# Two edits in the expert phase: a multiply moves from VectorE to Pool, and a reload moves from SyncE's queue to ScalarE's

## The reference, cut to what matters

```python
def block(xc):                                    # 128 tokens at a time
    q = (xc @ w_q).reshape(PEER_BLOCK, PEER_HEADS, 2, PEER_KEY_DIM // 2)
    s = jnp.einsum("chsd,hskd->chsk", q, keys)
    top_s, top_i = lax.top_k(s, PEER_TOPK)
    ...                                           # the best 16 of 16 x 16 pairs, for each of 8 heads
    e = i1 * PEER_NKEYS + i2                      # 128 of 16384 experts per token
    g = jax.nn.softmax(best_s, axis=-1)
    act = jax.nn.gelu(jnp.einsum("cd,chkd->chk", xc, u_tab[e]))
    return jnp.einsum("chk,chkd->cd", g * act, v_tab[e])

x = x + g_f * peer_ffn(modulate(rmsnorm(x, norm_ffn_w[i]), sh_f, sc_f), ...)
```

## Time and profile before

| | |
|---|---|
| time, median of 3 runs | 3000.66 us (2999.98 to 3004.64) |
| the profiled execution's own time | 2996.64 us |
| its span, first to last instruction | 2994.8 us |
| granted TensorE clock, mean | 0.946 |
| busy share: TensorE, VectorE, Pool, ScalarE | 88%, 70%, 42%, 24% |
| moved by DMA | 917.84 MB, mean 306 GB/s |
| of it by the gathers' queue / the queue of plain DMAs | 536.94 MB / 378.73 MB |

### The profile page before, as it was taken

The page is one execution under the profiler, slowest core; times in us unless marked ns, Lnnn a source line. Parts: engine busy times, 40 slices in busy tenths (PEclk is TensorE's granted clock), DMA queues, the critical chain, the costliest instruction groups (busy, mean ns, idle before and its releaser), DMA issues. The chain is left out here.

```text
span 2994.8 us, 36163 instructions
## 1 busy us (share of the span) xinstructions
PE 2631.8 (88%) x12550; PEld 2163.9 (72%) x12550; DVE 2099.4 (70%) x4541; ACT 706.4 (24%) x1947; POOL 1246.7 (42%) x1028
## 2 busy tenths in 40 slices
PE   4789869999999996999966878999999998899993
PEld 2544558888888885888854756888888886688882
DVE  2365248989979866666674346989989976666666
ACT  2345142234444300000004424213444410000000
POOL 0000000546557765555650000164656765556662
PEclk7888989999999998999987988999999999899996
DMA  7156122899999999999991213499999999999995
GB/s 297 64 216 266 56 100 65 326 349 367 360 375 409 408 409 404 409 409 409 409 365 63 77 56 121 148 385 323 369 362 409 408 407 406 408 409 409 409 409 205
DMA packets 246587, 917.84 MB, mean 306 GB/s; under 512 B 27120, under 2 KB 32272, under 8 KB 239120
## 3 DMA queue, kind: packets, MB, share of 16 engines
q0 software_dynamic: 147456, 536.94, 45.9%
q1 hardware_dynamic: 98960, 378.73, 33.0%
HBM read 909.27 MB, written 6.29 MB: 306 GB/s over the span
## 5 line engine op out<-in xcount | busy, mean ns | idle before, releaser
L1093 POOL DMA_INDIRECT all_xT<-in_u_rows,peer_eidx x296 | 375.7, 1269 | 1127.2 <-DVE peer_eidx L1436 879.0
L1164 PE MATMUL exp_down<-peer_gates,all_ring 128*128 128x256 f32 x2720 | 619.7, 385 | 72.3 <-DMA all_ring<-in_peer_v 72.1
L1164 PEld LDWEIGHTS exp_down<-peer_gates,all_ring 128*128 128x128 f32 x2720 | 512.0, 191 | 170.0 <-DMA all_ring<-in_peer_v 102.2
L1136 PE MATMUL exp_out<-peer_hd,all_ring 128*128 128x256 f32 x2752 | 616.0, 380 | 12.6 <-DMA all_ring<-in_uT 6.6
L1136 PEld LDWEIGHTS exp_out<-peer_hd,all_ring 128*128 128x128 f32 x2752 | 516.5, 190 | 89.9 <-DMA all_ring<-in_uT 14.3
L1518 DVE SCALAR_TENSOR_TENSOR peer_hs<-all_xT,peer_dots,peer_hs 128x1024 f32<-128x1024 f32 x226 | 290.5, 1285 | 144.5 <-DMA all_xT<-in_peer_v,peer_eidx 141.4
L1511 DVE CUSTOM_DVE_ANT_0 all_xT<-all_xT,peer_hs 128x1024 f32<-128x1024 f32 x296 | 359.5, 1220 | 42.7 <-DMA all_xT<-in_u_rows,peer_eidx 41.6
L1093 POOL DMA_INDIRECT all_xT<-in_peer_v,peer_eidx x228 | 261.7, 1148 | 178.4 <-DVE peer_hs L1518 154.2
L1164 PE MATMUL exp_down<-peer_gates,spare_ring 128*128 128x256 f32 x1376 | 314.4, 381 | 8.2 <-DMA spare_ring<-in_peer_v 8.2
L1136 PE MATMUL exp_out<-peer_hd,spare_ring 128*128 128x256 f32 x1344 | 305.5, 380 | 8.0 <-DMA spare_ring<-in_uT 4.4
L1164 PEld LDWEIGHTS exp_down<-peer_gates,spare_ring 128*128 128x128 f32 x1376 | 257.8, 190 | 53.8 <-DMA spare_ring<-in_peer_v 19.2
(11 more groups left out here) (293 smaller groups left out, 3700.8 us busy)
## 6 DMA issues: line engine op xcount, KB each, us to landing
all_ring<-in_uT SPq DMA_DIRECT2D x172, 512.0 KB, 6.8
all_ring<-in_peer_v SPq DMA_DIRECT2D x170, 512.0 KB, 6.8
mix_raw<-in_ada_tiles SPq DMA_DIRECT2D x48, 1024.0 KB, 9.8
spare_ring<-in_peer_v SPq DMA_DIRECT2D x86, 512.0 KB, 6.8
spare_ring<-in_uT SPq DMA_DIRECT2D x84, 512.0 KB, 6.7
all_ring<-in_w_peer_q SPq DMA_DIRECT2D x22, 512.0 KB, 3.8
all_ring<-in_w_gs_in SPq DMA_DIRECT2D x16, 512.0 KB, 3.7
all_ring<-in_w_in SPq DMA_DIRECT2D x12, 512.0 KB, 3.8
```

The source lines that it names most:

```text
L1093: nc.gpsimd.indirect_dma_start(out=rows[j], out_offset=None, in_=table, in_offset=bass.IndirectOffsetOnAxis(ap=q.eidx[:, b, k:k + 1], axis ...
L1136: mm = nc.tensor.matmul(outs[:, c % 2, 0:DENSE], raw[c % R][:, k, :], hd[:, k, :], start=(k == 0), stop=(k == KD - 1))
L1164: mm = nc.tensor.matmul(dn[:, m, :], raw[at % R][:, m, :], gates[:, :, c, :], start=(c == 0 and m % 2 == 0), stop=(c == NKEYS - 1), skip_g ...
```

## The change

`post` goes from VectorE's stream to Pool's. Pool executes it after it has issued gather i + 9, where VectorE executed it after slot i. The two reloads go from SyncE's stream to the end of ScalarE's, behind `gelu_dots(1)`, which waits for slot 255, and behind two waits: for the last `up` tile and for the last post.

```diff
         @block.sync
...
-                if c == NKEYS + 24:
-                    sp.wait_ge(s_post, len(POST))
-                    sp.dma_start(q.back[:, :, :], x_dram[:, :, PICKED:SEQ]).then_inc(s_back, 16)
-                    sp.dma_start(hd[:, :, :], x_dram[:, :, 0:PICKED]).then_inc(s_back, 16)
-            sp.wait_ge(s_back, 32)
         @block.gpsimd
         def _(pool):
+            def post(p):
+                pool.wait_ge(s_act, 2 * p + 2)
+                pool.wait_ge(s_gev, sum(after < p for after in GATES_AFTER))
+                held, (n0, n1), pair = q.acts[p % 4], known(p), slice(2 * p, 2 * p + 2)
+                if n1 == P:
+                    cut = gates[:, :, pair, :].rearrange("p b c n -> p b (c n)")
+                    last = nc.gpsimd.tensor_tensor(cut, cut, held[:, :, :, :].rearrange("p b c n -> p b (c n)"), ALU.mult)
+                else:
+                    cut = gates[:, 0, pair, 0:n0]
+                    last = nc.gpsimd.tensor_tensor(cut, cut, held[:, 0, :, 0:n0], ALU.mult)
+                    if n1 > 0:
+                        cut = gates[:, 1, pair, 0:n1]
+                        last = nc.gpsimd.tensor_tensor(cut, cut, held[:, 1, :, 0:n1], ALU.mult)
+                last.then_inc(s_post, 1)
...
                 nc.gpsimd.indirect_dma_start(
                     out=rows[j], out_offset=None, in_=table,
                     in_offset=bass.IndirectOffsetOnAxis(ap=q.eidx[:, b, k:k + 1], axis=0)).then_inc(s_row[j], 16)
+                if n - 9 in POST_AT:
+                    post(POST_AT[n - 9])
         @block.scalar
...
             gelu_dots(1)
+            act.wait_ge(s_mm, NKEYS)
+            act.wait_ge(s_post, len(POST))
+            act.dma_start(q.back[:, :, :], x_dram[:, :, PICKED:SEQ]).then_inc(s_back, 16)
+            act.dma_start(hd[:, :, :], x_dram[:, :, 0:PICKED]).then_inc(s_back, 16)
+            act.wait_ge(s_back, 32)
         @block.vector
...
-            def post(p):
...
-                if i in POST_AT:
-                    post(POST_AT[i])
```

## The result

The changed kernel takes 3035.09 us (median of 4 runs, 3030.7 to 3040.37) beside 3002.26 us for the kernel before on the same chip: ratio 1.0114, 95% interval 1.0101 to 1.0127, so 34 us slower. Forecast were 3028 us, 27 above the median, and a range of 2985 to 3070. The profiled execution of after took 3030.7 us, span 3028.9.

A forecast was written before the change was run, and what follows sets the result against it. VectorE's row chain was taken to end the expert phase last, by about 23 us. (1.5 + 4) x 0.69 + 9 x 0.85 + 2.1 = 13.6 us per layer, 27 for both, gave 3000.66 + 27 = 3028 us, range 2985 to 3070.

The forecast's parts named there:

- Where the bound lies: Expert phase: VectorE-bound, then Pool and latency, then DMA, then VectorE, whose row chain ends last by about 23 us.
- The reload, +2.1 a layer: Reload on ScalarE's queue: dense stream ends about 24 us earlier, gathers are made up at the tail, +2.1 us per layer.
- TensorE's stall was the bound: Rival, at the reload around 1134 us: 27.5 us a layer come back, 2946 us; chance 0.03.
- 641 to 800, +1.5: First window, VectorE setting the pace: it is held 7.6 us and sheds 6.1, +1.5 us per layer.
- The hold: VectorE two-input SBUF operations and Pool instructions reading SBUF wait for one another; 0.38 us average wait per gather from 870 to 1070.
- 800 to 870, +4: Second window, Pool late: five posts cost 6 us there, less the 2 VectorE sheds, +4 us per layer.
- 870 to 1070, +9 before the factor: Third window, DMA full: Pool has 21.6 us spare, the posts need 50, 28 too much; +9 us per layer taken.
- I take a third of the 28: Third window: gathers' own waiting shrinks as VectorE starves and pays the rest of Pool's excess, leaving +9 us.
- The factor from a late row to the end, 0.85: Third window to phase end: each us lost by gathers costs 0.85 us at the end, half-way from 0.69 to 1.
- Pool is free and VectorE is not held: Rival, first and third windows: VectorE's shed work is gained, -6.9 us a layer, 2987 us; chance 0.20.
- Pool's queue in full: Rival, third window: all 28 us of Pool's excess count, 29.7 us a layer, 3060 us; chance 0.18.
- It cancels out: Rival: the first window's gain and small losses on Pool stay within 6 us in all; chance 0.14.

The follow-up runs named there:

- e6: Kernel before with each post on Pool writing zeros over the held columns instead of multiplying, reload on SyncE: 2995.55 us, ratio 0.9986.
- e10: Kernel before with every second post from pair 42 on moved to Pool, the others on VectorE, reload on SyncE: 3006.15 us, ratio 1.0016.
- e8: Kernel before with all posts on Pool but multiplying only a quarter of their columns, reload on SyncE: 3006.18 us, ratio 1.0016.
- e11: Kernel before with nothing moved; Pool also writes zeros to a scratch buffer, 53 writes a layer at the late posts' places: 3024.89 us, ratio 1.0068.
- e7: Kernel before with Pool writing four times as many byte zeros in place of each post's multiply, reload on SyncE: 3022.88 us, ratio 1.0067.
- e12: Kernel before with nothing moved; Pool also does scratch multiplies reading two SBUF inputs at the late posts' places: 3039.47 us, ratio 1.0114.
- e4: Kernel before with only the posts from pair 42 on moved to Pool, the others on VectorE, reload on SyncE: 3022.29 us, ratio 1.009.
- e1: Kernel before with all posts moved to Pool as in the change, the reload left on SyncE: 3030.86 us, ratio 1.0119.
- e2: Kernel before with only the reload moved to ScalarE's queue, the posts left on VectorE: 3001.24 us, ratio 1.0014.
- e3: Kernel before with only the posts up to pair 33 moved to Pool, the others on VectorE, reload on SyncE: 2994.62 us, ratio 0.9994.
- e5: Kernel before with the posts' multiplies left out, Pool only waiting and counting at their places, reload on SyncE: 2995.97 us, ratio 0.9984.
- e9: Kernel before with a second multiply on VectorE behind each multiply of the posts from pair 42 on, Pool untouched: 3000.47 us, ratio 0.9996.

## Why it came out so, step by step

The runs of the third window in one table. "Added" is the busy time of what was put on Pool between 870 and 1070 us in the profile, "too much" is that less the 21.6 us that the prediction found spare, and the cost is per layer, half of the measured one.

| kernel | reads SBUF | added us | too much | cost per layer |
|---|---|---|---|---|
| e6, short writes | no | 12.0 | none | -2.1 |
| e10, every second late post | yes | 24.5 | 2.9 | 2.4 |
| e8, a quarter of the columns | yes | 25.3 | 3.7 | 2.4 |
| e11, scratch writes beside | no | 36.8 | 15.2 | 10.2 |
| e7, long writes | no | 37.9 | 16.3 | 10.0 |
| e12, scratch multiplies beside | yes | 39.3 | 17.7 | 17.1 |
| e4, late posts | yes | 40.8 | 19.2 | 13.5 |
| e1, all posts | yes | 40.3 | 18.7 | 17.9 |
| the change | yes | 42.2 | 20.6 | 17.1 |

Two things are shown. The cost is not proportional to what is added: 12 us cost nothing, 25 cost 2.4 a layer, 37 about 10. And by this table each us too much costs 0.61 to 0.67 us where nobody is held, and 0.65 to 0.97 where the added work reads SBUF. e1, e7, e8 and the change hold the cost of the posts of 800 to 870 as well, and what VectorE gains by having no posts; e11 and e12 hold neither.

Where the bend lies is less sure than the 21.6 looks. Only e6 lies well below it, and the 21.6 are of one window of one profile: in the second layer's (2259 to 2459) Pool is busy 139.41 us with 111 gathers, which leaves 27.3 spare. Counted from there e8 and e10 would be under the threshold in that layer, and each us above it would cost more.

*Where the bound lies.* Right. Rows come late from the third window on, the row chain still ends last, and the second part of the phase neither adds nor gives back much: 18.1 us late at the 256th row, 16.6 at the last.

*The reload, +2.1 a layer.* Right alone: e2 has +4.2 us for both layers. TensorE waits 5.3 us in after around the reload and 5.0 in e2. I allowed 3 for new stalls; with 2 to 4 us per 100 us of such waits elsewhere, that was not too little. One reading in the working was loose: the 847 packets of the earlier trace rows carry 3.08 MB, 3.6 KB each, so some are small, and an estimate that puts all the time on 4 KB ones gives 0.17 us for one and 168 GB/s for SyncE's queue in place of 190. That is still above 147, and nothing changes. The rival that TensorE's stall was the bound is refuted. On top of the posts the reload shows nothing: 34 us with it, 36 without, within the intervals. I gave TensorE's lead as 45 us; it is 46.4 in e2, and 50.8 in after, where the rows come later.

*641 to 800, +1.5.* The hold is there, as e3's rows show (1231 against 1221 ns, 467 against 424), and the sum is zero: e3 measured -1.8 us for both layers, with zero inside its interval. But this zero doesn't prove the hold. The 6.1 us that VectorE was to gain without it were too many: in e5 nothing is held, its rows gain 2 to 3 us there and lose them to the wait for ScalarE. So the near hit of this term is in part luck.

*800 to 870, +4.* Not tried alone. By subtraction 5 a layer remain, 3.5 either way; the forecast's 4 x 0.69 = 2.8 lies inside.

*870 to 1070, +9 before the factor.* This is the term that was mis-sized, and its errors ran against each other. The need was put at 50 us: 12.3 of issue, 22 of work, 15.6 of waiting. Measured are 42.2 in all; a multiply needs none of a gather's 0.30 us of issue (idle before the multiplies: 0.3 us in all), and costs 1.08 us with its wait against the 0.92 taken. So 20.6 us are too much, not 28. But of these I let the gathers' own waiting pay two thirds, and it paid hardly anything. By the window's busy time (where instructions overlap, it counts once) they take 129.8 / 101 = 1.285 us against 1.32, 3.7 us over the window; by the groups' own sums 132.7 / 101 = 1.31 against 146.2 / 110 = 1.33, under 2. That leaves 17 or more, and 9 gathers fewer at 200 / 110 = 1.82 us each say about the same, 16.4. **The step that failed is "I take a third of the 28": it was four fifths of 21.** I had the waiting shrink because VectorE starves. In after it hardly does: the hold keeps it busy for 168.74 us where it was 174.97. And where it does starve, for 44 us in e7, the gathers still take 1.33 us on average. One cause is to be seen in the trace of before: the 34 gathers that start when VectorE frees their buffer take 1.23 us on average, the 76 that start after "issue" 1.37, and in after 97 of the 101 are of the second kind. That this is the whole of it is not shown.

*Luck in the total.* The forecast of 27 us is nearer to the 34 than its largest term was: this window was put at 9 x 0.85 = 7.7 us a layer, and e4 measured 13.5.

*The factor from a late row to the end, 0.85.* 16.6 us at the end for 18.1 at the 256th row is 0.92, with the reload in it. Without the reload, in e1, VectorE's rows are 21.2 and 20.7 us late at the 256th slot and 17.0 and 17.4 near the last: 0.80 and 0.84. The factor was about right.

*The hold.* It exists in both directions. The Trainium skill (SBUF - State Buffer, Who interferes with whom) says that the exclusion holds against Pool's reads and not against instructions that only write; the traces agree: beside writes VectorE's row operation stays at 1224 ns (e7), beside reads its mean rises to between 1291 and 1421 ns by buffer in after. But its price is not where I first looked for it. Over the third window of after, the 102 row operations take 134.0 us in place of 102 x 1.221 = 124.5, the 56 one-hots 28.0 in place of 23.7: the hold stretches VectorE by 14 us, about the 14.6 that it sheds, and e9 put 9.8 us more on VectorE in that window for nothing. What costs is mostly that Pool's own instructions are long. The hold adds to it twice: it lengthens Pool's multiply, and, with Pool full, reading costs some us a layer beyond that: about 4 by e12 against e11, about 6 by e1 against e7 (17.9 - 10.0, less 1.6 for 2.4 us more on Pool), each uncertain by 3. That these come from VectorE's stretching is argued from the one-hots (515 against 419 ns) and not tried by itself; e9 loads VectorE by less (9.8 us) and with Pool not full.

*The rivals.* "Pool is free and VectorE is not held": both halves are refuted, the first by e7 and e11, the second by the stretched operations of after. "Pool's queue in full", 3060: too much, since its 28 us were. The truth lies between it and the forecast. "It cancels out": true for the first window only.

Summed as measured, per layer: 0 + 5 + 13.5 + (0 to 2) = 18.5 to 20.5, against 17.1 for the change; the pieces don't add exactly, the middle one being itself a difference.

No version that does all the multiplies beats the kernel before by more than can be measured. e5, with the multiplies left out altogether, gains 0.16%; e3, the part of the change that does no harm, 0.06% with zero in its interval.

## What to carry to other kernels

Before work is moved to a queue that issues DMAs, add up that queue over the stretch where the transfers are the bound (busy time plus issue), and treat what is spare as a rough threshold: here 12 us on a queue with 21.6 spare were free, and well above it 0.6 us or more of each came back at the end. Price the moved instruction with its waits on the new engine (here 1.08 us for what took 0.36), and don't count on the waits of the others to shrink. And ask what the engine that is relieved was worth: leaving the work out altogether answers that in one run, and here the answer was 0.16%.

## What the runs showed of the hardware

- Pool's multiply of two f32 SBUF operands: 0.73 us at the least for 256 columns in the third window, 1.06 on average beside VectorE; 1.29 for the one of 512. VectorE took 0.418 for 256. The Trainium skill's ratio (GPSIMD Engine Reference, Performance versus the Vector engine) gave an estimate of 0.8 us for 256 columns, a little nearer to 0.73 than the 0.63 that my 1.5 times VectorE's 0.418 makes.
- Pool's write of zeros: 331 ns for 256 f32 columns, 538 for 512, 800 for 832 bytes, 970 for 1024 (e6, e7, e11). The same 1024 bytes take 331 ns as 256 elements and 970 as 1024, and VectorE's row operation stays at 1224 ns beside it.
- A multiply of 64 columns beside VectorE takes 0.73 us on average and 0.33 at the least (e8): over a half of its price is waiting.
- A gather on Pool takes 0.94 us with nothing in its way. In the third window of the first layer its mean is 1.31 to 1.34 us in before, after, e7, e11 and e12, whether VectorE is busy for 156 or for 175 of the 200 us.
- A reload in 1 KB packets on a queue of its own leaves TensorE 5 us of small waits in 110 us, of which 2 to 4 are there without it, where in front of the tiles on their queue it cost 24.66 at one place. Moving it from the one place to the other shifts the end by 2 us a layer (e2).
